# Router logits from column groups of TensorE: the router matrix as the stationary side, and a fold by a 0/1 matrix

## The chip, the cores and the metric

The kernel runs on one core of one Trainium2 chip, in one launch. The metric is the device time of an execution in microseconds (us); the median of several runs is compared. In the profile PE is TensorE (matmul), PEld its weight loads, ACT is ScalarE, DVE is VectorE, POOL is GpSimd, and SP the engine that issues the weight transfers.

## The reference, cut to what matters

A decoder trunk of four layers on 256 tokens of 1024 features, all float32. Each layer has a token mixer (gated DeltaNet, differential attention, gMLP, gated DeltaNet again) and then a mixture of 16 experts with 512 hidden features, of which each token uses two. The router matrix is the same in all layers.

```
def grouped_moe(h, w_router, router_bias, w1, w3, w2):
    scores = sigmoid(h @ w_router)                    # (256, 1024) @ (1024, 16)
    sel = scores + router_bias
    # best of 4 groups by the sum of its two highest; two experts in that group
    # gates = their scores over their sum
    out = sum over e of gates[:, e] * ((silu(h @ w1[e]) * (h @ w3[e])) @ w2[e])

for i in range(4):
    h = layer_norm(ALPHA * h + mixer_i(h))
    h = layer_norm(ALPHA * h + grouped_moe(h))
```

The change touches `h @ w_router` alone.

## The kernel before

Each engine runs a program written out by hand, and the engines meet at semaphores. The eight PSUM banks (128 x 512 float32 each) pass from TensorE to a reader and back: `fill(key)` makes TensorE wait until the bank of that key is drained, `done` reports it filled, `wait_data` lets a reader wait for that, `emptied` reports it drained, and `wait_copy` waits for the drained report. The table behind it, `plan`, counts the turns of each bank in program order. Weights stream from HBM through a ring of six buffers of 2 MB, in the order of their use, and a buffer is loaded again when TensorE is through with it.

Around a router the order is this. Behind the mixer, VectorE normalises the 256 tokens (L986). TensorE turns them into eight chunks of 128 features by 256 tokens, one in each PSUM bank (`ht_chunks`, L1506): first all chunks of the first 128 tokens, then of the second. ScalarE copies the even chunks (L626) and VectorE the odd ones (L946) to HT, with the gain and offset of the norm. For each chunk k TensorE then multiplies it with the router matrix `wr` (L1815), once per half of the tokens: HT is the stationary side (128 columns are loaded), `wr[:, k, :]` the moving side (16 columns are streamed), and the sixteen products add up in bank 0, tokens in the partitions. ScalarE, having copied its chunks, loads its table for exp with a small exp ahead of need (L633), and then takes exp of the 128 x 32 logits (L867). VectorE makes the sigmoid of it, ranks the experts and writes a mask (`route`, L1271 to L1294). TensorE counts with the mask (L1822 to L1824), VectorE turns the counts to places, and TensorE gathers the tokens of the first two experts (L1830) and goes into the loop over eight pairs of experts (L1841 is the first pair of its products, in two column groups of 64: w1 and w3).

Every float32 product shows in the profile as two records, each with its own weight load. A product whose output starts at another partition than 0 uses other columns of the array: a column group.

At the start ScalarE issues some twenty small transfers (L618), the router matrix among the last, and GpSimd sets constants in memory (L508 to L511). A semaphore counts these, `params_in` the transfers.

## Time and profile before

| | us |
|---|---|
| median of 3 runs | 2081.63 (2077.19 to 2081.88) |
| the profiled execution | 2074.54 |
| its span | 2072.8 |
| TensorE busy | 1884.8 (91%) |
| VectorE, ScalarE, GpSimd busy | 718.7, 500.9, 160.6 |

The span runs from the first to the last instruction of the profiled execution. TensorE's clock has two levels, shown as the granted clock: 1.00 is 2.4 GHz, 0.50 is 1.2 GHz; its mean here is 0.943. A router comes four times, near 260, 717, 1255 and 1800 us.

### The profile page before, as it was taken

To read this page: it belongs to the slowest core of one execution; us is meant where nothing else is said; L and a number is where in the kernel's file an instruction comes from. 1 tells how busy PE (TensorE), PEld (TensorE's weight loads), DVE (VectorE), ACT (ScalarE), POOL (GpSimd) and SP (SyncE) were. 2 spreads that over 40 slices of the span, in tenths; PEclk is the share of its full clock that TensorE was granted. 3 is DMA by queue.
4 is the path that set the end of the run, shared out by engine and by line. 5 is a ranking of instruction groups with operands and counts; after the bars stand their busy time and mean duration, and the time that the engine had idled before them with its cause. 6 is when DMAs were issued, how large, how long until landed. Compare 5 with 4: busy or idle time off the path is not lost. (4 is left out here: it accounts for less than half of the span.)

```text
span 2072.8 us, 28488 instructions
## 1 busy us (share of the span) xinstructions
PE 1884.8 (91%) x10610; PEld 1047.6 (51%) x10611; DVE 718.7 (35%) x1433; ACT 500.9 (24%) x1002; POOL 160.6 (8%) x96
## 2 busy tenths in 40 slices
PE   8998979999895789889989997899979988899997
PEld 7858554443763444344434544434438758544442
DVE  3435443232305552223323115232323434543233
ACT  1655221121104111111121101121113745112211
POOL 1112021000300030000020002100002120020000
PEclk9999989999995899989999998899999999889999
DMA  9321149999730266548994424679994330269994
GB/s 356 137 82 64 60 187 410 426 427 404 268 127 35 81 265 260 199 179 356 427 367 148 162 81 174 277 322 423 426 394 155 118 107 3 82 273 428 421 428 194
DMA packets 80056, 504.46 MB, mean 243 GB/s; under 512 B 7171, under 2 KB 11444, under 8 KB 55100
## 3 DMA queue, kind: packets, MB, share of 16 engines
q1 hardware_dynamic: 69808, 488.65, 58.6%
q0 software_dynamic: 2304, 8.39, 1.1%
q10 hardware_dynamic: 7820, 5.65, 0.9%
q8 instruction: 92, 1.51, 0.3%
q14 instruction: 32, 0.26, 0.0%
HBM read 501.61 MB, written 1.06 MB: 243 GB/s over the span
## 5 line engine op out<-in xcount | busy, mean ns | idle before, releaser
L1841 PE MATMUL bank<-ring,work 128*64 128x512 f32 x2176 | 484.3, 603 | 11.6 <-DVE work L1382 6.0
L1841 PEld LDWEIGHTS bank<-ring,work 128*64 128x64 f32 x2176 | 155.6, 139 | 331.0 <-issue 323.8
L1859 PE MATMUL bank<-ring,work 128*64 128x512 f32 x1088 | 244.2, 596 | 9.2 <-ACT work L897 4.6
L1515 PE MATMUL bank<-HT,ring 128*128 128x256 f32 x1024 | 231.3, 386 | 2.9 <-DMA ring<-in_a_w_in 2.9
L1515 PEld LDWEIGHTS bank<-HT,ring 128*128 128x128 f32 x1024 | 198.2, 194 | 39.9 <-issue 10.2
L1523 PE MATMUL bank<-ring,HT 128*128 128x512 f32 x448 | 196.9, 600 | 0.0
L1368 DVE TENSOR_TENSOR work<-bank,work 64x512 f32<-64x512 f32 x64 | 68.0, 1062 | 323.2 <-ACT work L875 323.0
L875 ACT ACTIVATE work<-bank 64x512 f32<-64x512 f32 x64 | 37.8, 590 | 524.7 <-PE bank L1841 524.7
L1830 PE MATMUL bank<-work 128*128 128x128 f32 x1024 | 141.2, 296 | 13.3 <-DVE work L1347 7.1
L1859 PEld LDWEIGHTS bank<-ring,work 128*64 128x64 f32 x1088 | 75.3, 137 | 148.9 <-issue 141.5
L1830 PEld LDWEIGHTS bank<-work 128*128 128x128 f32 x1024 | 129.4, 206 | 38.7 <-issue 29.3
L1523 PEld LDWEIGHTS bank<-ring,HT 128*128 128x128 f32 x448 | 85.8, 193 | 104.8 <-issue 104.7
L1337 DVE TENSOR_TENSOR work<-bank,lncols 128x512 f32<-128x512 f32 x64 | 44.3, 692 | 268.6 <-PE bank L1830 268.6
L1958 PE MATMUL bank<-work 128*128 128x512 f32 x256 | 115.6, 594 | 7.7 <-ACT work L891 5.9
L891 ACT ACTIVATE work<-bank 64x512 f32<-64x512 f32 x128 | 75.8, 592 | 183.3 <-PE bank L1859 182.6
L1062 DVE SCALAR_TENSOR_TENSOR work<-bank,convcols,work 128x255 f32<-128x255 f32 x144 | 69.3, 482 | 105.9 <-ACT work L691 102.5
L1415 DVE TENSOR_TENSOR H<-bank,H 128x512 f32<-128x512 f32 x128 | 84.6, 686 | 52.4 <-PE bank L1958 52.0
L1548 PE MATMUL bank<-ring,work 128*128 128x512 f32 x192 | 85.7, 605 | 0.0
L1958 PEld LDWEIGHTS bank<-work 128*128 128x128 f32 x256 | 46.2, 190 | 57.4 <-issue 57.4
L553 POOL TENSOR_TENSOR H<-H,gB 128x1024 f32<-128x1024 f32 x6 | 14.0, 2356 | 759.8 <-PE bank L1506 759.8
L550 POOL TENSOR_TENSOR H<-work,gB 128x1024 f32<-128x1024 f32 x8 | 23.1, 2905 | 584.2 <-DVE work L1342 584.2
L1548 PEld LDWEIGHTS bank<-ring,work 128*128 128x128 f32 x192 | 36.8, 194 | 44.9 <-issue 44.9
(271 smaller groups left out, 1805.7 us busy)
## 6 DMA issues: line engine op xcount, KB each, us to landing
ring<-in_e_w SPq DMA_DIRECT2D x192, 2048.0 KB, 13.3
ring<-in_a_w_in SPq DMA_DIRECT2D x16, 2048.0 KB, 14.7
ring<-in_c_w_in SPq DMA_DIRECT2D x8, 2048.0 KB, 14.2
ring<-in_b_w_in SPq DMA_DIRECT2D x6, 2048.0 KB, 15.9
ring<-in_a_w_out SPq DMA_DIRECT2D x4, 2048.0 KB, 8.3
ring<-in_c_w_out SPq DMA_DIRECT2D x4, 2048.0 KB, 7.9
ring<-in_b_w_out SPq DMA_DIRECT2D x2, 2048.0 KB, 7.9
gB<-in_ln_mix_g POOLq DMA_DIRECT2D x4, 512.0 KB, 4.2
```

The source lines that it names most:

```text
L891: ins = a(y_[CAP * j:CAP * (j + 1), nh * 512:(nh + 1) * 512], bank[b][nh * CAP:(nh + 1) * CAP, :], ACT.Copy)
L1062: ins = v.scalar_tensor_tensor(dst[:, back:SEQ], ps[:, 0:SEQ - back], convcols[:, j, col:col + 1], dst[:, back:SEQ], ALU.mult, ALU.add)
L1337: v.tensor_tensor(sl, bank[g][:, :].rearrange("p (k c) -> p k c", k=4), lncols[:, g_col + 4 * g:g_col + 4 * g + 4].unsqueeze(2).to_broadca ...
L1368: v.tensor_tensor(by_m(h_[j]), bank[b][CAP:, :], sil[j][CAP:, :], ALU.mult).then_inc(drained[b], 1)
L1415: v.tensor_tensor(part(b), bank[b][:, :], part(b), ALU.add).then_inc(drained[b], 1)
L1515: ins = mm(dst[:, 0:SEQ], wt[:, k, n * P:(n + 1) * P], HT[:, k, :], start=k == 0, stop=k == KC - 1)
L1523: ins = mm(dst[:, :], HT[:, k, tt * P:(tt + 1) * P], wt[:, k, :], start=k == 0, stop=k == KC - 1)
L1548: ins = mm(ps[:, :], turned(h, tt), wts[nh][:, h, :], start=h == 0, stop=h == HEADS - 1)
L1830: ins = mm(bank[g][:, k * 2 * CAP:(k + 1) * 2 * CAP], XH[:, tt, (4 * g + k) * P:(4 * g + k + 1) * P], sel[:, tt, :], start=tt == 0, stop=t ...
L1841: ins = mm(bank[b][lo:lo + CAP, :], x[:, k, :], wt[:, k, :], start=k == 0, stop=k == KC - 1, skip_group_check=True)
L1859: ins = mm(bank[b][nh * CAP:(nh + 1) * CAP, :], h[:, m, :], w2[:, m, nh * 512:(nh + 1) * 512], start=m == 0, stop=m == 3, skip_group_check ...
L1958: mm(bank[b][:, :], selgT[:, tt * P:(tt + 1) * P], y_[:, nh * 512:(nh + 1) * 512], start=True, stop=True).then_inc(filled[b], 1)
```

## The change

The router matrix becomes the stationary side and HT the moving side. Each chunk k is now one product: 32 columns of `wr` are loaded (16 of the matrix and 16 zeros), 256 tokens are streamed, and the result lies in 32 partitions of bank 2, one of four groups by k modulo 4. Chunks k and k + 4 add up in the same group. ScalarE copies the four parts (128 partitions, 256 tokens) to `logitT`. Two products with `logitT` as the stationary side and a 0/1 matrix `fold` as the moving one add the four parts and put the tokens back in the partitions, in bank 0, where exp reads them as before.

```diff
+C_FOLD = C_IOTA + 2 * CAP
+C_SB = C_FOLD + E
...
         if with_moe:
+            turns.take(2, "rtq", i)
             turns.take(0, "rt", i)
...
-        wr = sb("wr", [P, KC, E])
+        wr = sb("wr", [P, KC, 2 * E])
...
+        logitT = work[:, 6144:6144 + SEQ]
...
+            pool.memset(wr[:, :, E:], 0.0).then_inc(consts_set, 1)
...
-            small.append((wr[:, :, :], w["w_router"].rearrange("(p k) n -> p k n", p=P)))
+            small.append((wr[:, :, 0:E], w["w_router"].rearrange("(p k) n -> p k n", p=P)))
...
-            act.wait_ge(consts_set, 4)
+            act.wait_ge(consts_set, 5)
...
             def experts(i):
                 ahead(ACT.Exp)
+                emptied(a(logitT, wait_data(act, "rtq", i)[:, 0:SEQ], ACT.Copy), "rtq", i)
                 emptied(a(rt[:, 0, :], wait_data(act, "rt", i)[:, 0:TT * E], ACT.Exp, scale=-1.0), "rt", i)
...
-                ps = fill("rt", i)
+                ps = fill("rtq", i)
                 for k in range(KC):
                     wait_copy(pe, "ht", 2 * i + 1, k)
-                    for tt in range(TT):
-                        ins = mm(ps[:, tt * E:(tt + 1) * E], HT[:, k, tt * P:(tt + 1) * P], wr[:, k, :],
-                                 start=k == 0 and tt == 0, stop=k == KC - 1, skip_group_check=True)
+                    q = slice(2 * E * (k % 4), 2 * E * (k % 4 + 1))
+                    ins = mm(ps[q, 0:SEQ], wr[:, k, :], HT[:, k, :], start=k < 4, stop=k >= 4, skip_group_check=True)
+                done(ins, "rtq", i)
+                ps = fill("rt", i)
+                wait_copy(pe, "rtq", i)
+                for tt in range(TT):
+                    ins = mm(ps[:, tt * E:(tt + 1) * E], logitT[:, tt * P:(tt + 1) * P], fold, start=True, stop=True)
                 done(ins, "rt", i)
...
+    c[:, C_FOLD:C_FOLD + E] = m % (2 * E) == np.arange(E)[None, :]
```

Word for word, TensorE's order at the first router, before: the last transposes, the sixteen router products (the first eight rows of them are shown), each `drained` being the bank of a chunk that must have been copied.

```order
L1506 MATMUL bank<-consts_sb,work 128x128 [waits xhat_ready]
L1506 MATMUL bank<-consts_sb,work 128x128 x3
L1815 MATMUL bank<-wr,HT 128x16 [waits drained0]
L1815 MATMUL bank<-wr,HT 128x16
L1815 MATMUL bank<-wr,HT 128x16 [waits drained1]
L1815 MATMUL bank<-wr,HT 128x16
L1815 MATMUL bank<-wr,HT 128x16 [waits drained2]
L1815 MATMUL bank<-wr,HT 128x16
L1815 MATMUL bank<-wr,HT 128x16 [waits drained3]
L1815 MATMUL bank<-wr,HT 128x16
```

The same place on TensorE now (line numbers are those of the changed kernel; L1832 is the first product with the mask):

```order
L1512 MATMUL bank<-consts_sb,work 128x128 x3
L1821 MATMUL bank<-HT,wr 32x256 [waits drained0,drained2]
L1821 MATMUL bank<-HT,wr 32x256 [waits drained1]
L1821 MATMUL bank<-HT,wr 32x256 [waits drained2]
L1821 MATMUL bank<-HT,wr 32x256 [waits drained3]
L1821 MATMUL bank<-HT,wr 32x256 [waits drained4]
L1821 MATMUL bank<-HT,wr 32x256 [waits drained5]
L1821 MATMUL bank<-HT,wr 32x256 [waits drained6]
L1821 MATMUL bank<-HT,wr 32x256 [waits drained7]
L1826 MATMUL bank<-consts_sb,work 128x16 [waits drained2,drained0]
L1826 MATMUL bank<-consts_sb,work 128x16
L1832 MATMUL bank<-work,consts_sb 128x32 [waits mask_ready,drained1]
```

Sixteen products have become eight and two; the first now waits for bank 2 too, and the two folding products wait for ScalarE's copy (`drained2`).

ScalarE at the same place before: its last two chunks, the table load, and the exp of the logits.

```order
L626 ACTIVATE HT<-bank,lncols 128x256 [waits filled4]
L626 ACTIVATE HT<-bank,lncols 128x256 [waits filled6]
L633 ACT_TABLE_LOAD
L633 ACTIVATE warm<-epsc 128x1
L867 ACTIVATE work<-bank 128x32 [waits filled0,a_chain]
```

ScalarE now:

```order
L631 ACTIVATE HT<-bank,lncols 128x256 [waits filled4]
L631 ACTIVATE HT<-bank,lncols 128x256 [waits filled6]
L638 ACT_TABLE_LOAD
L638 ACTIVATE warm<-epsc 128x1
L872 ACTIVATE work<-bank 128x256 [waits filled2,a_chain]
L873 ACTIVATE work<-bank 128x32 [waits filled0]
```

The copy (L872) stands between the warm-up and the exp, and no further table load comes with it.

## Rows read from the trace of the kernel before

**Rows 1.** Page: busy time of each engine, share of the span, instructions.

```profile
PE 1884.8 (91%) x10610; PEld 1047.6 (51%) x10611; DVE 718.7 (35%) x1433; ACT 500.9 (24%) x1002; POOL 160.6 (8%) x96
```

**Rows 2.** Chain of waits, layer 3's router: start us, us, what.

```profile
1800.75 5.61 PE bank L1815 x32
```

**Rows 3.** Timeline, layer 0's router: start us, us, instructions [idle before].

```profile
259.41 1.93 ACT L626 ACTIVATE HT<-bank,lncols 128x256 f32<-128x256 f32 x4 [2.11 <-PE bank L1506]
...
260.65 6.85 PE L1815 MATMUL bank<-wr,HT 128*128 128x16 f32 x32
...
262.65 0.20 ACT L633 ACTIVATE warm<-epsc 128x1 f32<-128x1 f32 x1
267.60 0.20 ACT L867 ACTIVATE work<-bank 128x32 f32<-128x32 f32 x1 [4.74 <-PE bank L1815]
```

**Rows 4.** Timeline, layer 1, from the router to the first experts.

```profile
716.14 1.93 ACT L626 ACTIVATE HT<-bank,lncols 128x256 f32<-128x256 f32 x4 [1.98 <-PE bank L1506]
...
716.92 4.27 PE L1815 MATMUL bank<-wr,HT 128*128 128x16 f32 x32
...
719.38 0.20 ACT L633 ACTIVATE warm<-epsc 128x1 f32<-128x1 f32 x1
721.28 0.20 ACT L867 ACTIVATE work<-bank 128x32 f32<-128x32 f32 x1 [1.70 <-PE bank L1815]
...
725.42 0.50 PEld L1822 LDWEIGHTS bank<-work,consts_sb 128*128 128x128 f32 x2 [4.35 <-issue]
...
726.23 0.55 PEld L1824 LDWEIGHTS bank<-work,ones 128*128 128x128 f32 x2
...
726.99 0.16 DVE L1304 CAST counts<-bank 1x16 int32<-1x16 f32 x1 [0.81 <-PE bank L1824]
...
728.56 6.14 PE L1830 MATMUL bank<-work 128*128 128x128 f32 x32 [1.67 <-DVE work L1347]
...
734.62 3.65 PE L1841 MATMUL bank<-ring,work 128*64 128x512 f32 x16
```

**Rows 5.** Timeline, layer 2's router.

```profile
1253.99 1.93 ACT L626 ACTIVATE HT<-bank,lncols 128x256 f32<-128x256 f32 x4 [1.98 <-PE bank L1506]
...
1257.24 0.20 ACT L633 ACTIVATE warm<-epsc 128x1 f32<-128x1 f32 x1
1260.94 0.20 ACT L867 ACTIVATE work<-bank 128x32 f32<-128x32 f32 x1 [3.50 <-PE bank L1815]
```

**Rows 6.** Timeline, layer 3's router.

```profile
1799.79 1.93 ACT L626 ACTIVATE HT<-bank,lncols 128x256 f32<-128x256 f32 x4 [1.98 <-PE bank L1506]
...
1803.04 0.20 ACT L633 ACTIVATE warm<-epsc 128x1 f32<-128x1 f32 x1
1806.44 0.20 ACT L867 ACTIVATE work<-bank 128x32 f32<-128x32 f32 x1 [3.20 <-PE bank L1815]
```

**Rows 7.** Stretches: length, busy us of each engine, granted clock, DMA share, GB/s.

```profile
718.00:720.00 2.00, 2.00 (x19) 2.00 (x19) 0.18 (x1) 1.56 (x3) 0.00 (x0) 0.94 0.37 156
1254.00:1256.00 2.00, 1.99 (x18) 1.75 (x16) 2.00 (x5) 1.98 (x5) 0.00 (x0) 0.91 1.01 434
1800.00:1802.00 2.00, 1.99 (x18) 1.91 (x17) 1.85 (x5) 1.98 (x5) 0.00 (x0) 0.94 1.03 442
```

**Rows 8.** Line L1515 in 14.4:19 and 35.8:43.9: ns min/median/max, first and last start.

```profile
L1515 PE MATMUL bank<-HT,ring x11: 634/634/796, 14.4 to 18.8; 128*128 128x256 f32 x11
...
L1515 PE MATMUL bank<-HT,ring x39: 379/379/379, 35.6 to 43.8; 128*128 128x256 f32 x39
```

**Rows 9.** Page, costliest groups: busy us, mean ns of one, idle before.

```profile
L1841 PE MATMUL bank<-ring,work 128*64 128x512 f32 x2176 | 484.3, 603 | 11.6 <-DVE work L1382 6.0
```

**Rows 10.** Line L773 in 1700:1730: a copy of 128x256 on ScalarE.

```profile
L773 ACT ACTIVATE work<-bank x2: 385/385/385, 1721.0 to 1721.5; 128x256 f32<-128x256 f32 x2
```

**Rows 11.** Timeline at the start of the kernel: GpSimd's first squares.

```profile
33.48 1.04 POOL L565 TENSOR_TENSOR work<-work 128x512 f32<-128x512 f32 x1 [17.85 <-DMA rel<-in_rel_bias]
...
35.60 1.04 POOL L565 TENSOR_TENSOR work<-work 128x512 f32<-128x512 f32 x1 [1.08 <-ACT work L681]
```

More of the change, by code:

```diff
@@ L58 @@
 C_IOTA = C_CD + 2 * E
-C_SB = C_IOTA + 2 * CAP
+C_FOLD = C_IOTA + 2 * CAP
+C_SB = C_FOLD + E
 C_OH = C_SB
@@ L227, in trunk @@
         tri = K_[:, C_TRI:C_TRI + P]
+        fold = K_[:, C_FOLD:C_FOLD + E]
         onehot = bB[0:REL_BUCKETS + 1, 0:TOEP]
@@ L1971, in _ @@
             pe.wait_ge(rows_for_cols, N_ROWS)
-            pe.wait_ge(consts_set, 4)
+            pe.wait_ge(consts_set, 5)
             ps = fill("cols")
```

## The prediction, made before the changed kernel ran

> **What bounds the kernel now.** I read four views in this order. First the page's busy times: TensorE (PE) is busy 91% of the span, 1884.8 us [rows 1]. That average doesn't say what the router logits are worth, so next the chain of waits at a router, in layer 3: the router products (L1815) stand in it with 5.61 us, nothing beside them [rows 2]. The work behind them is a string of short VectorE steps that all wait for ScalarE's exp (L867), so each microsecond by which that exp starts earlier is one of the whole. Third, the timeline at each of the four routers, for what ScalarE does meanwhile [rows 3 to 6]. The exp starts at 267.60, 721.28, 1260.94 and 1806.44 us; ScalarE has been free, its exp table warm (end of the 0.20 us at L633), since 262.85, 719.58, 1257.44 and 1803.24. The gaps are 4.75, 1.70, 3.50 and 3.20 us, 13.15 together: the most that any faster router product can give, before anything is added.
>
> The gaps differ because TensorE's clock does. In layer 0 the 32 records of L1815 take 6.85 us, 0.21 each; in layer 1 they take 4.27 [rows 3, 4]. The fourth view, stretches of 2 us with the granted clock, says why: 0.94 over 718 to 720 is the full level (1.00, 2.4 GHz) until 719.76 and the low one (0.50, 1.2 GHz) after it; 0.91 over 1254 to 1256 puts the fall at 1255.64, 0.94 over 1800 to 1802 at 1801.76 [rows 7]. Layer 0's block is as slow throughout as the low level makes it.
>
> Does the expert stage behind the router take a gain back? TensorE's waits there name VectorE, ScalarE and issue, no DMA. A router that ends earlier moves everything behind it earlier, the release of weight buffers too.
>
> **The change, part by part.** Removed per layer: 16 products, 32 records, each loading 128 columns of HT and streaming 16 of the router matrix. Added on TensorE: 8 products (16 records) that load 32 columns and stream 256, in four column groups in turn, and then two 128x16 products (4 records) that fold. Added on ScalarE between them: a copy of 128x256 out of PSUM, queued behind the table load and warm-up, with the exp behind it. Moved: the first router product now waits for bank 2 too, so for ScalarE's second HT chunk, where it waited for the first only.
>
> *A 256-column record.* At the low clock one lasts 634 ns, at the full clock 379, and there 39 start in 8.2 us, 0.216 each [rows 8]. Eleven at the low clock start over 4.4 us, 0.44 each, with one odd one among them; twice the full pitch is 0.43. I use 0.427 and 0.214. That is the price where one waits for the other.
>
> *Do column groups overlap?* The experts' products (L1841) alternate two groups of 64 columns, 512 streamed. Their 2176 records keep TensorE busy for 484.3 us, 0.223 each, though one lasts 603 ns and a record of 512 columns alone in the array would hold it twice 0.214 [rows 9]. So two run at a time. A product has two records in the same group, and they are issued in order, so what overlaps is the second half of one product with the first half of the next. Four groups in turn have the same order; I take one product per record time, 0.427 low or 0.214 full: twice as fast as in a row, not four times.
>
> *Start.* ScalarE's four chunks take 1.93 us at some 0.57 each, so pitch 0.455, and the second ends 1.02 after the first starts. In layer 1 the first chunk ended about 716.71 and the first product began at 716.92 [rows 4]: 0.2 us. New start: first chunk's start + 1.22.
>
> *Tail.* If TensorE ends last: 0.10 to ScalarE, 0.385 for a copy of this size [rows 10], 0.10 back, and the fold. For the fold rows 4 have four equal records at the low clock, loads from 725.42 to 726.23, 0.81 us, for two products; the reader of the last pair comes 0.76 after that pair's first load, so two products cost 0.81/2 + 0.76 = 1.17 us. Sum 1.75. If ScalarE ends last: 0.02 + 0.385 + 0.10 + 1.17 = 1.67 after its table is warm. The later of the two sets the exp. The copy could cost up to the 0.57 of an HT chunk, which carries a scale and a bias: 0.2 more per layer, 0.7 in all. I take 0.385, the like operation.
>
> - Layer 0, low clock: start 260.63, eighth product 7 x 0.427 later at 263.62, its second record 264.05, end 264.68, exp 266.43. Before 267.60: -1.17 us.
> - Layer 1, full clock: start 717.36, last record 719.07, end 719.45; ScalarE is free only at 719.58, exp 721.25. Before 721.28: -0.03.
> - Layer 2: start 1255.21, two products until the fall, then low: last record 1258.2, end 1258.84, exp 1260.59. Before 1260.94: -0.35.
> - Layer 3: start 1801.01, three and a half products until the fall: last record 1803.68, end 1804.31, exp 1806.06. Before 1806.44: -0.38.
>
> Sum -1.9 us. Of the 5 to 7 us block that went, most is given back by the later start (0.46 a layer), the copy (0.385) and the fold (1.17).
>
> *A switch between one array and column groups* comes twice per layer more. The trace has such a switch between the gather (L1830, 128 columns, ends 734.70) and the experts' first product (64 columns, starts 734.62): the next starts before the last ends [rows 4], so I take 0. Upper bound: the 0.2 us by which a record outlasts its pitch at the low clock (634 - 427 ns), eight times, 1.7 us. The Trainium skill (TensorEngine Tiling (Array Packing), Key Properties) says that changing the tiling mode drains TensorE; by that rule the sum would be about -0.2 instead of -1.9. The row shows no stop of that size.
>
> *At the start* the router matrix lands in pieces of 16 elements instead of runs of 128, the constants grow by 16 columns, and GpSimd gets one more memset. The last parameter lands before 33.48 us, where GpSimd begins its squares; its second squares begin at 35.60, after waiting 1.08 us for ScalarE [rows 11]. A landing up to 1 us later is hidden by that wait. Beyond it GpSimd still has most of its time free, and TensorE and ScalarE ask for parameters after 40 us. Bounds 0 and +1; I take 0.
>
> **Against the measured time.** The profiled execution took 2074.54 us for a span of 2072.8, so the sum makes 2072.6 of it. The median shown is 2081.63, 7 us above (2077.19 to 2081.88). Forecast: 2081.63 - 1.9 = 2079.7 us. About 0.3%, 6.2 us, is what a measurement of this kernel tells from no change.
>
> **Rivals.**
> 1. *The column groups don't overlap* (slower). Sixteen records stand in a row, full pitch until the fall, low after it: the last starts at 267.04, 721.4, 1261.2 and 1806.7; with 0.634 and 1.75 the exp is at 269.4, 723.8, 1263.6 and 1809.1: +1.8, +2.5, +2.6, +2.6 = +9.5 us, 2091.1. For it: nothing in this trace runs four groups, or groups of 32 columns. Against: two groups do overlap. It decides from a low-clock pitch per product of 0.427 + 1.9/28 = 0.50 us (seven steps in each of four layers), where the gain is gone; at 0.72 it is beyond 0.3%.
> 2. *The dense streaming keeps the clock up* (faster). The old block streams 16 columns a record, and the clock fell within it in three layers. If the new block runs at 2.4 GHz, ScalarE's queue alone sets the exp, 1.67 after its table is warm: 264.52, 721.25, 1259.11, 1804.91: -3.1, 0, -1.8, -1.5 = -6.4 us, 2075.2. With the fold at the full clock too, its four pitches and its last record take some 0.5 us less each: -8.4, 2073.2. Against it: the low level holds from the very beginning of layer 0's block, in a stretch that isn't touched, and the idle gaps before and behind the block stay. The Trainium skill (TensorE: Matmul & The Clock Gate, Part 1) says that the clock is throttled by default and that activity releases it, which is this rival's ground.
> 3. *The later start, the copy and the fold eat exactly what the products give*: no difference, 2081.6. All its parts are in the forecast; 1.9 us more of them are enough (the drain alone would be). For a reader of times it is the forecast's own answer.
>
> A spread, not a rival: where the clock rises again behind the router moves from one execution to the next. A record costs up to 0.1 us more at the low level [rows 3, 4], some 15 records per layer are at stake, so 1 to 2 us of either sign in a layer, and 2 in a median.
>
> **Chances.** Forecast 0.60, rival 3 0.21, rival 1 0.10, rival 2 0.09. Rival 2 passes the 0.3% with its first part just barely and with both; the spread can carry the forecast over it a few times in a hundred; of rival 1 nearly all lies beyond it. Faster 0.11, same 0.78, slower 0.11. The range runs from rival 2's far end to half way to rival 1: 2073.8 to 2086.0 us; the forecast's own is 2077 to 2083.
>
> **What would show it.** Right: first product behind ScalarE's second chunk; sixteen records within about 3.5 us at the low clock, one product every 0.43; the copy 0.4 us long; from copy to exp 1.3 us; in layer 1 the copy right behind the warm-up. Wrong: records 0.43 apart (rival 1); a granted clock of 1.00 through the blocks of layers 2 and 3 (rival 2); records of one product overlapping, or three products at a time, which would make the block shorter than I allow and leave ScalarE as the only bound; a gap of half a microsecond between transposes and router products (the drain); TensorE waiting for parameters in the first 60 us.

## The result, and the profile after

| | before | after |
|---|---|---|
| median of 9 runs, us | 2077.19 (2073.31 to 2081.88) | 2065.57 (2060.59 to 2073.05) |
| span of the profiled execution, us | 2072.8 | 2058.8 |
| four routers, ScalarE's first HT copy to its exp, us | 26.9 | 19.0 |

The ratio is 0.9932 [0.9909, 0.9954]: 0.7% faster, 11.6 us between the medians and 14.0 between the spans. The forecast was 2079.7 us, with a range down to 2073.8. It started from 2081.63, the median of three runs, where nine give 2077.19; beyond that its gain of 1.9 us is some 10 us too small.

The page after: TensorE's busy time fell by 18 us from that of [rows 1], and it has 48 records fewer.

```profile
span 2058.8 us, 28401 instructions
PE 1866.4 (91%) x10562; PEld 1024.9 (50%) x10563; DVE 717.8 (35%) x1433; ACT 502.1 (24%) x1006; POOL 160.0 (8%) x97
...
L1851 PE MATMUL bank<-ring,work 128*64 128x512 f32 x2176 | 485.3, 604 | 12.0 <-DVE work L1388 6.0
```

The experts' products are what they were [rows 9]. Now the timeline at layer 0's router, which answers to [rows 3] (start us, length, instructions, in brackets the idle time before and what ended it; L1821 is the new block, L872 the copy, L1826 the fold, L873 the exp):

```profile
261.36 1.93 ACT L631 ACTIVATE HT<-bank,lncols 128x256 f32<-128x256 f32 x4 [1.97 <-PE bank L1512]
262.43 0.27 PEld L1821 LDWEIGHTS bank<-HT,wr 128*32 128x32 f32 x8 [0.35 <-ACT HT L631]
262.43 1.65 PE L1821 MATMUL bank<-HT,wr 128*32 128x256 f32 x16
...
264.60 0.20 ACT L638 ACTIVATE warm<-epsc 128x1 f32<-128x1 f32 x1
264.84 0.38 ACT L872 ACTIVATE work<-bank 128x256 f32<-128x256 f32 x1
265.37 0.59 PE L1826 MATMUL bank<-consts_sb,work 128*128 128x16 f32 x4 [1.28 <-ACT work L872]
265.99 0.20 ACT L873 ACTIVATE work<-bank 128x32 f32<-128x32 f32 x1 [0.77 <-PE bank L1826]
...
273.35 6.58 PE L1840 MATMUL bank<-work 128*128 128x128 f32 x32 [1.76 <-DVE work L1353]
```

All sixteen records are through in 1.65 us, 0.1 us a record on average; the old block took 6.85. TensorE ends at 264.08, before ScalarE is free at 264.80. From there copy, fold and exp follow in 1.19 us. In layer 2 the clock falls within the block; this answers to [rows 5]:

```profile
1248.09 2.10 PE L1821 MATMUL bank<-HT,wr 128*32 128x256 f32 x16
...
1250.27 0.20 ACT L638 ACTIVATE warm<-epsc 128x1 f32<-128x1 f32 x1
1250.50 0.38 ACT L872 ACTIVATE work<-bank 128x256 f32<-128x256 f32 x1
1251.03 1.00 PE L1826 MATMUL bank<-consts_sb,work 128*128 128x16 f32 x4 [0.83 <-ACT work L872]
1252.07 0.20 ACT L873 ACTIVATE work<-bank 128x32 f32<-128x32 f32 x1 [1.18 <-PE bank L1826]
```

Even here the block ends (1250.19) before ScalarE is free (1250.47); only the fold is slower, 1.00 instead of 0.59. The granted clock, as in [rows 7] (after the clock: DMA share, GB/s):

```profile
262.00:264.00 2.00, 1.89 (x19) 0.87 (x17) 1.41 (x4) 1.98 (x4) 0.00 (x0) 1.00 0.98 418
...
1247.00:1249.00 2.00, 1.87 (x18) 1.08 (x17) 2.00 (x5) 1.96 (x5) 0.00 (x0) 0.88 1.01 434
1250.00:1252.00 2.00, 1.17 (x6) 0.92 (x4) 0.00 (x0) 0.84 (x3) 0.00 (x0) 0.50 1.05 451
...
1786.00:1788.00 2.00, 1.87 (x20) 1.20 (x20) 1.78 (x4) 1.98 (x5) 0.00 (x0) 1.00 1.05 451
```

Full level (1.00, 2.4 GHz) through the block in layers 0 and 3, where the old block had the low one all through or from 1801.76 on; in layer 2 it falls to 1.2 GHz within the block. Layer 1 is the other way round: its block begins at the low level, which by the two stretches lasts until about 719.45, and yet takes 1.68 us:

```profile
716.27 1.57 PEld L1512 LDWEIGHTS bank<-consts_sb,work 128*128 128x128 f32 x8 [1.83 <-DVE work L992]
...
716.78 1.93 ACT L631 ACTIVATE HT<-bank,lncols 128x256 f32<-128x256 f32 x4 [2.12 <-PE bank L1512]
...
718.17 0.20 PEld L1821 LDWEIGHTS bank<-HT,wr 128*32 128x32 f32 x8 [0.33 <-ACT HT L631]
718.17 1.68 PE L1821 MATMUL bank<-HT,wr 128*32 128x256 f32 x16
```

```profile
716.00:718.00 2.00, 1.73 (x8) 1.57 (x8) 1.88 (x5) 1.22 (x3) 0.00 (x0) 0.51 1.05 451
...
718.00:720.00 2.00, 1.85 (x18) 0.77 (x16) 0.90 (x2) 1.98 (x3) 0.00 (x0) 0.64 0.56 238
```

Where the 14.0 us went, from the timelines and windows of the two traces (in brackets the same for a second pair of executions, whose spans differ by 17.7):

| stage | before | after | difference |
|---|---|---|---|
| start to layer 0's router | 259.4 | 261.4 | +2.0 (+4.0) |
| four routers, first HT copy to exp | 26.9 | 19.0 | -7.9 (-9.1) |
| exp to the experts' first product | 53.4 | 54.1 | +0.7 (0.0) |
| experts | 1117.4 | 1111.8 | -5.6 (-9.6) |
| mixers | 615.6 | 612.7 | -2.9 (-2.9) |

Two things call for an explanation: 8 us at the router where 1.9 were forecast, and 8 to 12 us less in the stages behind the routers, among instructions that the change doesn't touch.

### The profile page after: what moved, and what is told of

Same layout as the page of the kernel before. It is cut to its first block and busy times, and to the rows that moved or that the text cites. A ratio compares the mean times of both kernels' runs of the same rounds, so it can differ in the third digit from the quotient of the medians.

```text
span 2058.8 us, 28401 instructions
## 1 busy us (share of the span) xinstructions
PE 1866.4 (91%) x10562; PEld 1024.9 (50%) x10563; DVE 717.8 (35%) x1433; ACT 502.1 (24%) x1006; POOL 160.0 (8%) x97
## 5 line engine op out<-in xcount | busy, mean ns | idle before, releaser
L1869 PE MATMUL bank<-ring,work 128*64 128x512 f32 x1088 | 245.5, 602 | 7.5 <-ACT work L903 4.6
L1869 PEld LDWEIGHTS bank<-ring,work 128*64 128x64 f32 x1088 | 76.7, 138 | 147.2 <-issue 139.7
## 6 DMA issues: line engine op xcount, KB each, us to landing
ring<-in_c_w_in SPq DMA_DIRECT2D x8, 2048.0 KB, 12.5
```

The source lines that it names most:

```text
L1869: ins = mm(bank[b][nh * CAP:(nh + 1) * CAP, :], h[:, m, :], w2[:, m, nh * 512:(nh + 1) * 512], start=m == 0, stop=m == 3, skip_group_check ...
```

## The experiments

Ratios are to before, from runs of the same job, with their 95% interval. "Router" is the second row of the table above.

### How many column groups

The change unchanged, and again with one and two groups of 32 columns in place of four; copy and fold are then of 32 or 64 partitions. The number of instructions doesn't change.

```diff
-q = slice(2 * E * (k % 4), 2 * E * (k % 4 + 1))
-ins = mm(ps[q, 0:SEQ], wr[:, k, :], HT[:, k, :], start=k < 4, stop=k >= 4, ...)
+q = slice(2 * E * (k % n), 2 * E * (k % n + 1))          # n = 1, n = 2
+ins = mm(ps[q, 0:SEQ], wr[:, k, :], HT[:, k, :], start=k < n, stop=k >= KC - n, ...)
```

> The changed kernel once more, beside the three variants of this series. The first execution moved the exp of the router, counted from ScalarE's first HT copy, from 8.19, 5.15, 6.95 and 6.65 us to 4.63, 4.63, 5.05 and 4.63: 8.0 us of the 14 by which the span fell; the other 6 us are spread over stretches that run the same instructions. Theory A (only the router block changed, and the other 6 us are where the clock's low stretches happened to fall): again 4.6 to 5.1 us per layer, a total 8 to 11 us below the kernel before. Theory B (the block also changes the clock of what follows, for good): 12 to 15 us below, and less low-clock time behind the routers in this trace too.

> All eight router products in the same column group of 32, so that nothing in the block can overlap; the copy and the fold take 32 partitions instead of 128. Theory 'the groups are what pays': sixteen records at 0.214 us (full clock) from 1.07 us after ScalarE's first copy on, end at 4.7, exp at 6.0 us at the full clock and up to 9.9 at the low one, against 4.6 to 5.1: 6 to 14 us slower than the changed kernel, near the kernel before. Rival 'it is the clock': dense streaming of 256 columns keeps the clock at 1.00 and the exp stays within 1.5 us per layer of the changed kernel, under 6 us in all.

> Two column groups instead of four; copy and fold take 64 partitions. If each group holds one record at a time and groups are free of each other, records start in twos, the block takes about 1.9 us at the full clock and ends before ScalarE's table is warm, so the exp stays at 4.6 us; at the low clock it ends about 4.7 us after the first copy and the exp comes at 6.4 instead of 5.0. Sum 0 to 4 us slower than the changed kernel. If, as I had forecast, a product's second half must go before the next product's first, two and four groups give the same block: no difference at either clock.

| groups | median us | ratio | router us | block at the full clock, us |
|---|---|---|---|---|
| 4 | 2065.27 | 0.9924 [0.9897, 0.9951] | 19.0 | 1.65 |
| 2 | 2064.58 | 0.9913 [0.9888, 0.9939] | 21.1 | 1.92 |
| 1 | 2075.06 | 0.9975 [0.9953, 0.9997] | 25.0 | 3.64 |

The kernel of after came out 16 us below before in this series. The theory that the untouched stages change by chance gave 8 to 11, the one that the block also changes the clock of what follows gave 12 to 15; TensorE's time at the low level is 217 us in this trace and 206 in the first, against 237 and 234 in the two traces of before.

Timeline of layer 1 with one group, then layers 1 and 2 with two:

```profile
716.60 3.64 PE L1821 MATMUL bank<-HT,wr 128*32 128x256 f32 x16
...
718.77 0.20 ACT L638 ACTIVATE warm<-epsc 128x1 f32<-128x1 f32 x1
720.33 0.37 ACT L872 ACTIVATE work<-bank 32x256 f32<-32x256 f32 x1 [1.36 <-PE bank L1821]
721.47 0.20 ACT L873 ACTIVATE work<-bank 128x32 f32<-128x32 f32 x1 [0.77 <-PE bank L1826]
```

```profile
722.45 1.92 PE L1821 MATMUL bank<-HT,wr 128*32 128x256 f32 x16
...
1252.24 3.31 PE L1821 MATMUL bank<-HT,wr 128*32 128x256 f32 x16
...
1255.65 0.38 ACT L872 ACTIVATE work<-bank 64x256 f32<-64x256 f32 x1 [1.04 <-PE bank L1821]
```

With one group ScalarE has the table warm at 718.97 and waits 1.36 us for TensorE; sixteen records at 0.214 and the last one's length make the 3.64. With two groups the block takes 1.92 at the full clock. Going from one group to four saves 6.0 us of router. From two to four it saves 2.1, because only where the clock is low does the shorter block still matter (3.31 us long in layer 2, ScalarE waits 1.04); the times of the two kernels don't differ. (The profiled execution of two_groups was 11 us longer than its median; I read nothing of it but the router and one pair of experts.)

So four groups do better than the two records at a time of the forecast, which would put the last start 7 x 0.214 = 1.5 us behind the first and the end at 1.9, what two groups take. How much better shows where the low level slows the array down. In layer 1 of after four records start within 0.02 us, the next four 0.43 us later, and so on. In the second trace of after (after_again) the whole block of layer 0 runs at the low level, and takes 1.94 us:

```profile
264.87 1.94 PE L1821 MATMUL bank<-HT,wr 128*32 128x256 f32 x16
```

```profile
264.00:266.00 2.00, 2.00 (x17) 1.32 (x19) 1.60 (x4) 1.98 (x5) 0.00 (x0) 0.50 0.99 426
```

Four products, not one, share a record time of 0.43 us, and both halves of a product do so. At the full clock the array isn't even the limit: the last four products of layer 0 each start some 0.05 us after their HT chunk is copied, so the 1.65 us are the pace of ScalarE's and VectorE's chunks. The Trainium skill (TensorEngine Tiling (Array Packing), Key Properties) says that tiles run independently, loads and products in parallel; the starts in fours agree with it.

One group alone changes the router by -1.9 to -3.1 us, and is 0.25% (5 us) faster. The interval of that ratio takes in 2 to 3 us as well, so it is no more than a hint at a second cause.

### ScalarE's copy moved to VectorE

```diff
-                emptied(a(logitT, wait_data(act, "rtq", i)[:, 0:SEQ], ACT.Copy), "rtq", i)
 ...
+                emptied(v.tensor_copy(logitT, wait_data(dve, "rtq", i)[:, 0:SEQ]), "rtq", i)
                 route(i)
```

> The copy of the four parts goes to VectorE, which is idle there, instead of ScalarE behind its table load. Theory 'ScalarE's queue is the bound now': block end 2.7 us after the first copy, plus 0.1, 0.42 (a copy of this size on VectorE), 0.1 and the fold 0.7 to 1.1: exp at 4.1 instead of 4.6 us, 2 us faster in all than the changed kernel. Rival 'TensorE's block or the fold is the bound': no difference in the exp's start.

Measured 2068.03 us, 0.9941 [0.9917, 0.9966]. Timeline of layer 1:

```profile
717.56 1.65 PE L1821 MATMUL bank<-HT,wr 128*32 128x256 f32 x16
...
719.25 0.42 DVE L1321 COPY work<-bank 128x256 f32<-128x256 f32 x1 [0.71 <-PE bank L1821]
719.73 0.20 ACT L638 ACTIVATE warm<-epsc 128x1 f32<-128x1 f32 x1
720.51 0.20 ACT L872 ACTIVATE work<-bank 128x32 f32<-128x32 f32 x1 [0.57 <-PE bank L1826]
```

VectorE copies while ScalarE still warms its table, and the exp comes 0.58 after the table instead of 1.19. The router falls from 19.0 to 16.5 us: ScalarE's queue was the bound in all four layers. But the time doesn't follow: where 2 us less than after was expected, no difference can be measured. A router time alone doesn't set the time of this kernel to within 3 us.

### Before, once more

> The kernel before, unchanged, for a second trace and the noise. All theories: ratio 1.000 within its interval. If the router block of before is really set by TensorE's weight loads, the exp comes 5 to 8.2 us after ScalarE's first HT copy in each layer, whatever the place of the clock's low stretches; if a value under 5 appears, the first trace was an unlucky one and the gain of the change is smaller than 8 us. The stretch up to the first router took 259.4 us against 260.5 to 266.5 in the five executions with the change: if the small transfers at the start cost something, this trace is again near 259; if it is chance, it lies among the others.

2080.31 against 2080.22 us, 1.0007 [0.9988, 1.0025]; router 28.1 us. Its four routers take 4.75, 8.19, 7.05 and 8.15 us where the first trace has 8.19, 5.15, 6.95 and 6.65; the sum is near, the layers change places. Those of after are 4.63, 4.63, 5.05 and 4.63 in both of its traces. The 4.75 is the old block at the full clock but for its last 0.6 us:

```profile
260.30 3.85 PE L1815 MATMUL bank<-wr,HT 128*128 128x16 f32 x32
```

Where the old block has the full clock, then, the change saves 0.1 us of router; where it has the low one throughout, 3.6. The new router takes 4.63 us at either level (layer 0 of after and of after_again). Four routers of 4.75 us would be 19.0, the sum of after: the 8 us are what the low clock cost the old block.

### Products that only keep TensorE busy

Ten products of 256 columns into a bank that nothing reads, seven behind the fold and three behind the ranks, while TensorE waits for VectorE; in before, in after, and in the version with VectorE's copy. The last kernel has four of 512 columns instead.

```diff
                 done(ins, "rt", i)
+                for _ in range(7):
+                    mm(bank[7][:, 0:SEQ], ones[:, :], K_[:, 0:SEQ], start=True, stop=True)
 ...
+                for _ in range(3):
+                    mm(bank[7][:, 0:SEQ], ones[:, :], K_[:, 0:SEQ], start=True, stop=True)
                 first = at[("moe", i)]
```

> The kernel before with products that nobody needs in TensorE's idle time of each router: seven of 128x256 behind the router products (while VectorE ranks) and three behind the ranks (they write a free bank). Theory 'the low clock behind the routers is the engine's idleness': the gather runs at the full clock, 4.1 us instead of 5.9 per layer, 6 to 7 us less in all, minus up to 2 us where the seven products, at the low clock, outlast VectorE's chain. Rival 'the clock there is chance': no difference.

> The same seven and three products in the changed kernel. If dense streaming keeps the clock up, it enters the idle time at 1.00 and stays there: gather 4.1 us instead of 5.6 to 6.5, ranks 0.4 us shorter: 7 to 10 us less than the changed kernel, about 2057 us where that has 2065. Rival: the clock falls anyway within the block of seven, and what they delay eats the gain: within 2 us of the changed kernel.

> After_fill with the copy on VectorE: exp 0.6 us earlier per layer as copy_dve's trace showed (4.02 instead of 4.63), so 2 us less than after_fill. If the times of copy_dve (2068 where the changed kernel had 2065) mean that VectorE's copy costs something later on, it is again slower than its partner by some 3 us.

> Filling products again, but three of 512 columns and one instead of seven and three of 256: 16 more instructions a layer than the changed kernel instead of 40, 2.6 and 0.85 us of streaming at the full clock. The clock theory expects from fold to experts the 6.7 + 3.9 us of after_fill instead of 7.3 + 6.0. Theory L adds only that the waits of the expert loops come out as some other mixture: 2055 to 2066 us. Without L it should be 8 us under the changed kernel, 2057.

| kernel | median us | ratio | router | exp to experts | experts |
|---|---|---|---|---|---|
| before_fill | 2084.96 | 1.0015 [0.9996, 1.0035] | 30.1 | 45.8 | 1125.8 |
| after_fill | 2071.42 | 0.9946 [0.9927, 0.9964] | 18.5 | 42.6 | 1125.2 |
| dve_fill | 2069.29 | 0.9928 [0.9901, 0.9954] | 17.5 | 42.9 | 1127.9 |
| after_fill512 | 2070.14 | 0.9929 [0.9907, 0.9952] | 19.0 | 43.9 | 1128.3 |

Timeline of after_fill, layer 3 (L1829 and L1877 the added products, L1842 the gather):

```profile
1801.28 3.27 PE L1829 MATMUL bank<-consts_sb,ones 128*128 128x256 f32 x14
...
1806.30 1.54 PE L1877 MATMUL bank<-consts_sb,ones 128*128 128x256 f32 x6
1808.12 3.84 PE L1842 MATMUL bank<-work 128*128 128x128 f32 x32 [0.28 <-DVE work L1353]
```

The gather runs at the full clock, 3.84 us instead of the 5.6 to 6.6 of after, and exp to experts shrinks by 11 us. None of it arrives: after_fill was expected near 2057 us and isn't faster than after, and its experts' stage is 9 to 13 us longer than in the two traces of after. Most of that is TensorE's busy time (6 to 11 us more over the same products), with 89 us at the low level in that stage instead of 69 and 80; the waits that the profile calls "issue" (the engine waited for nothing that it shows) grow by 1 to 2 us. So the experts' stage isn't independent of what stands ahead of it.

### Padding: more instructions, nothing else

N products of 32 x 8 behind the fold, into the same unread bank: 4 instructions each (two loads, two matmuls). The change removes 24 instructions per layer, so N = 6 puts the number of before back, and N = 10 has as many as after_fill.

```diff
                 done(ins, "rt", i)
+                for _ in range(N):
+                    mm(bank[7][0:32, 0:8], ones[:, 0:32], K_[:, 0:8], start=True, stop=True)
```

> Two of the short products, 8 more instructions a layer. Theory L: the short first pairs of 25.9 us in layers 1 and 2 may be kept or lost, one of them at least differs from after_pad6 or the changed kernel, and the time lies between 2060 and 2072. Rival C: no difference to the changed kernel, 2065 within 2 us.

> The changed kernel with six products of 32 columns by 8 behind the fold, in the 4.3 us in which TensorE waits for VectorE's ranks: 24 more instructions a layer, as many as the change took out, so that from there on the program lies where it lay before. They are short enough not to delay the ranks. In both traces of the kernel before, the first pair of experts in layers 1 and 2 took 29.9 to 32.3 us; in all five of the change and its variants with as few instructions 25.9 to 26.6; in the three with the filling products 29.4 to 31.5. Theory L (where the program's instructions lie decides at which branches TensorE waits for them): first pairs of layers 1 and 2 back at 30 us and some 3 to 9 us slower than the changed kernel, 2068 to 2074 us. Rival C (the clock's phase, or the earlier exp, makes them short): 25.9 us as in the changed kernel, same time.

> Ten of the short products, 40 more instructions a layer: the same place for the program as in after_fill, without the clock that the long ones kept up. Theory L: first pairs of layers 1 and 2 at 30 us, last pairs at 33 to 35 as in after_fill, and a time 7 to 10 us above after_fill (2071), about 2079 us, though TensorE's routers are those of the changed kernel. Rival C: as the changed kernel, 2065.

> The kernel before with six of the short products behind the router products of each layer, in TensorE's wait for the ranks: nothing on the path to the exp. Theory L (the place of the program decides part of the time): the experts' first and last pairs come out otherwise than in the kernel before, and the time differs from it by up to 8 us of either sign. Rival: what the short products cost in after_pad6 and after_pad10 is theirs alone (they delay the ranks or lower the clock): then also the kernel before gets 8 to 10 us slower, with first and last pairs as before.

| kernel | instructions per layer against before | median us | ratio | router |
|---|---|---|---|---|
| after | -24 | 2065.27 | 0.9924 [0.9897, 0.9951] | 19.0 |
| after_pad2 | -16 | 2070.11 | 0.9948 [0.9927, 0.9968] | 18.5 |
| after_pad6 | 0 | 2075.84 | 0.9961 [0.9938, 0.9983] | 19.0 |
| after_pad10 | +16 | 2080.63 | 0.9990 [0.9967, 1.0013] | 18.5 |
| before_pad6 | +24 | 2090.62 | 1.0050 [1.0027, 1.0073] | 24.7 |

Timeline of after_pad10, layer 3:

```profile
1813.78 0.80 PE L1829 MATMUL bank<-consts_sb,ones 128*32 128x8 f32 x20
1813.89 0.20 ACT L873 ACTIVATE work<-bank 128x32 f32<-128x32 f32 x1 [0.77 <-PE bank L1826]
...
1818.05 0.61 PE L1834 MATMUL bank<-work,consts_sb 128*128 128x32 f32 x2 [3.47 <-DVE work L1300]
```

The padding is over in 0.8 us, beside the exp, and TensorE then waits 3.47 us for VectorE: on the spot it costs nothing, and the router keeps its 4.63 us in every layer. Yet the whole gain is gone. It is hardly the clock: over all executions the mean granted clock is 0.947 to 0.948 in after, 0.947 in after_pad6 and 0.946 in after_pad10, and within one kernel 0.001 of it goes with some 1.3 us. One place where the time goes is the first pair of experts. TensorE in layer 1, before, after and after_pad10 in turn (before's L1859 is after's L1869):

```profile
751.13 0.72 PE L1830 MATMUL bank<-work 128*128 128x128 f32 x5 [0.48 <-issue]
...
752.27 3.65 PE L1859 MATMUL bank<-ring,work 128*64 128x512 f32 x16
...
758.87 1.94 PE L1859 MATMUL bank<-ring,work 128*64 128x512 f32 x8 [2.94 <-issue]
```

```profile
749.09 2.05 PE L1840 MATMUL bank<-work 128*128 128x128 f32 x16
...
751.57 7.09 PE L1869 MATMUL bank<-ring,work 128*64 128x512 f32 x32
```

```profile
761.57 0.33 PE L1860 MATMUL bank<-consts_sb,work 128*128 128x128 f32 x1 [2.66 <-issue]
...
774.51 3.47 PE L1842 MATMUL bank<-work 128*128 128x128 f32 x16 [2.55 <-issue]
```

Windows over that whole first pair of experts, before and after:

```profile
734.62:765.10 30.48, 26.57 (x140) 11.41 (x140) 15.89 (x14) 4.78 (x11) 11.64 (x6) 1.00 0.71 287
```

```profile
734.55:760.40 25.85, 25.85 (x139) 11.24 (x139) 15.86 (x14) 4.65 (x10) 11.62 (x6) 1.00 0.65 262
```

Same work, same clock, but before has 3.91 us in which TensorE has no record, all of it "issue" (0.48 and 2.94 in the rows, 0.49 once more at 764.21), and after has none. In after_pad10 5.2 of the 7.0 us that the pair is longer than in after are "issue"; there the clock is low for 3.4 us too. Over all kernels the length of this pair goes with the program, not with the router:

| layer 1, first pair | us |
|---|---|
| before, before_again | 30.5, 30.6 |
| after, one_group, two_groups, copy_dve and the two staged versions below without filling | 25.9 each |
| after_pad2, after_pad6, after_pad10 | 26.1, 30.4, 32.9 |
| before_fill, after_fill, dve_fill, after_fill512 | 29.6, 30.4, 31.5, 30.1 |
| stage_dve_fill (16 instructions fewer than before) | 25.9 |
| before_pad6 | 31.5 |

With 16 or 24 instructions fewer than before the pair takes 26 us, with 8 fewer, as many or more 29.6 to 32.9. But this pair isn't the whole stage. From before to after the first pairs of all four layers together lose 7.3 us (11.7 in the second traces) and the last pairs gain 5.3 (7.3). Over the whole execution TensorE's "issue" waits are 23.9 and 26.4 us in the two traces of before, 26.9 and 26.1 in after, 30.2 in after_pad6, 33.6 in after_pad10 and 31.6 in before_pad6. before_pad6 is 0.50% slower than before (10 us, where up to 8 of either sign were expected). By the rival, that the short products cost something only where they stand, its first and last pairs had to be as before; its last pairs are 13 us longer in all.

So this much is shown: instructions that cost nothing where they stand, added to TensorE's program, make the kernel slower, in three doses in after and once in before. With the number of before the change keeps 0.39% of its 0.76%, some 8 us, which is what the routers gave. That the other half came by taking 24 instructions out follows from this comparison alone; the "issue" waits didn't become fewer from before to after, what fell in the experts' stage is TensorE's busy time (by 4 to 5 us, with 6 us less at the low level).

What TensorE waits for in these gaps the traces do say in part. The page has a DMA queue "q8 instruction", which moved 92 pieces of 16 KB in before. Over all 18 traces 206 "issue" waits of TensorE are longer than 1 us, and 197 of them end 1.2 to 2.4 us after the last landing of such a piece; of 990 equally long waits for another engine or a DMA it is 49. The 2.94 us of before lie around the piece that starts at 756.4. TensorE's instructions arriving late is what this points to, and a longer program shifts where the pieces end. It's a match in time; no run varied it by itself.

The fill kernels now read differently. after_fill and after_pad10 have equally many instructions; they differ by 9.2 us in median, and by 9.7 in exp to experts. The full clock for the gather is worth its 9 us, and 40 more instructions per layer, with the clock that the experts' stage loses, cost as much.

### The start of the kernel

The router matrix lands whole, in runs of 128 elements as before, in a tile of its own; GpSimd spreads it.

```diff
-small.append((wr[:, :, 0:E], w["w_router"]...))
+small.append((wr0[:, :, :], w["w_router"]...))
             pool.wait_ge(params_in, N_PARAMS)
+            pool.tensor_copy(wr[:, :, 0:E], wr0[:, :, :]).then_inc(consts_set, 1)
```

(TensorE waits for that sixth count at its first router.) Then the same with VectorE's copy, and that with two filling products of 512 columns.

> The changed kernel with one part undone: the router matrix lands in one run per partition, in a tile of its own, and GpSimd copies it to its places among the zeros once the parameters are in. In the five and more traces of the change GpSimd's first squares start at 38.7 to 39.9 us instead of 33.5 to 34.3, and the token products of the first gate begin at 112.9 us at the earliest instead of 111.9 to 112.5. Theory S (the scattered landing costs): squares at 34 us, first router 1 to 2 us earlier than in the change's traces, a time 1 to 2 us less. Rival (hidden, as I had forecast): squares earlier, the rest as it is.

> After_stage with the copy of the four parts on VectorE. By what the traces show of each part: exp at 4.0 us instead of 4.6 per layer (-2.4 us) and -1 us at the start, so 3 us below the changed kernel. As the changed kernel and copy_dve differ by +3 us where the parts say -2, I expect the place of ScalarE's and VectorE's programs to matter by as much: 2058 to 2068.

> Stage_dve with two products of 512 columns behind the fold, 8 more instructions a layer, 1.7 us of streaming at the full clock. If that is enough to keep the clock at 1.00 into the gather, gather and ranks are 2.5 us shorter a layer, 10 us in all; it is less than the 3.0 and 2.6 us that did. 2052 to 2066 us.

| kernel | median us | ratio | to layer 0's router | router |
|---|---|---|---|---|
| after_stage | 2062.69 | 0.9920 [0.9889, 0.9951] | 259.4 | 18.9 |
| stage_dve | 2065.74 | 0.9915 [0.9885, 0.9944] | 258.9 | 16.9 |
| stage_dve_fill | 2066.32 | 0.9929 [0.9906, 0.9952] | 261.8 | 16.6 |

GpSimd at the start, after and then after_stage, which answer to [rows 11]:

```profile
39.32 2.04 POOL L570 TENSOR_TENSOR work<-work 128x512 f32<-128x512 f32 x2 [23.94 <-DMA rel<-in_rel_bias]
```

```profile
34.45 0.29 POOL L588 COPY wr<-wr 128x128 f32<-128x128 f32 x1 [18.83 <-DMA rel<-in_rel_bias]
34.71 2.03 POOL L571 TENSOR_TENSOR work<-work 128x512 f32<-128x512 f32 x2
```

The last parameter lands near 39 us in after against 33.5 before, and near 34.4 with the whole matrix landing at once; the start stage falls by 2 us in the profiled executions. Its length also varies with the clock (259.9 to 269.4 us over the traces with the scattered landing), so TensorE's idle time up to the router is the better measure: 24.1 and 24.5 us in the traces of before, 25.7 and 25.9 in after, 24.5 in after_stage. The scattered landing costs some 1.5 us. after_stage has the lowest median, 2062.69 (2058.04 to 2071.13), and the shortest span, 2056.1. That it beats after isn't shown: the intervals overlap almost wholly. VectorE's copy on top brings nothing again, and the two filling products in stage_dve_fill, expected to bring up to 10 us, shorten exp to experts by 2 us and the time not at all.

## Why the prediction was wrong, step by step

**The overlap of column groups** is the step that failed: "I take one product per record time, 0.427 low or 0.214 full: twice as fast as in a row, not four times." The expert stage, with two groups, allowed both "two records at a time" and "as many as there are groups"; I argued from the order of a product's halves that four groups could do no better than two. It was four times: at the low level the block took 1.94 us (layer 0 of after_again), where the forecast had about 3.5 for the sixteen records; at the full one 1.65, the pace of the HT chunks. The prediction had named this outcome as a sign ("three products at a time, which would make the block shorter than I allow and leave ScalarE as the only bound"), and gave it no case and no chance. With ScalarE the bound in every layer my own numbers give -6.4 us (rival 2's sum), whatever the clock of the block.

**The clock.** Rival 2 (0.09) came half true: layers 0 and 3 had 1.00 through the block, layer 2 fell within it, and layer 1 had the low level for the first 1.3 of its 1.68 us. It didn't matter to the exp, since TensorE ended before ScalarE in all four. In layers 0, 1 and 3 the fold ran at the full clock: 1.19 us from warm table to exp where I had 1.67. In layer 2 it is 1.60. That is 3 x 0.48 + 0.07 = 1.5 us, and with the -6.4 makes the -7.9 of the table. One group, sixteen records in a row, had 1.00 throughout layer 1's block as well:

```profile
716.00:718.00 2.00, 1.89 (x11) 1.02 (x11) 1.59 (x4) 1.98 (x5) 0.00 (x0) 1.00 1.02 434
718.00:720.00 2.00, 2.00 (x11) 0.91 (x9) 0.00 (x0) 0.96 (x2) 0.00 (x0) 1.00 0.04 16
```

But its phase moves by itself: layer 0's router begins at the low level in before and in after_again, at the full one in after and in before_again. Over all executions after and its variants without padding or filling have a mean granted clock of 0.946 to 0.949, before has 0.942; by the 1.3 us for 0.001, some 7 of the 11 to 16 us go with it, the routers' own share included. Whether the dense block raised it or the shorter low stretches of a faster router count for it stays open.

**Copy and start of the block: right.** Copy 0.38 (forecast 0.385), from copy to exp 1.15; first load 1.07 after ScalarE's first HT copy at the full clock, 1.4 at the low one (1.22 forecast).

**Mode switch: 0 in the time, but not in the trace.** At the full clock TensorE's first load in 32-column groups starts 0.05 us after ScalarE's second HT chunk, so nothing of a stop shows. At the low level it does: in layer 1 of after the chunk is copied by 717.81 and the last load of the transposes over by 717.84, and the first load comes at 718.17, 0.33 us later; all blocks that begin at the low level have this gap. In before, without a switch, the first router load at the low level starts right with the end of the transposes' last (layer 0: within 0.02 us). The rule of the Trainium skill that was weighed there (TensorEngine Tiling (Array Packing), Key Properties: changing the mode drains TensorE) agrees with these 0.3 us. The row that spoke against it doesn't: the next record's start 0.08 us before the last one's end is what layer 1 shows as well (718.17 and 718.24), with the stop in it. The stop is longer than the 0.2 us that the prediction allowed for as its bound. It cost nothing because ScalarE ended last.

**Rival 1** (no overlap, +9.5) is refuted twice: by the overlap, and by one_group, where the products do stand in a row and the kernel is still not slower, since sixteen records at the full clock cost 3.64 us.

**The start** was mis-sized: 0, bound +1. The last landing moved by 5 us, not by up to 1, and the stage is 2.0 us longer, some 1.5 of it TensorE's idle time; after_stage gives the 2.0 back in its trace.

**What I had no term for**: the number of instructions. The forecast took the stages behind the router as fixed in length. They lost 7.8 us in this pair of traces (+0.7, -5.6, -2.9), 12.5 in the other, and by the padding 24 instructions per layer account for about half of the gain: after_pad6 is 0.37% above after, at the same mean clock. The page of before had the hint, "issue" as a cause of idle in the experts' stage, and I noted it without a price.

**The range** has slips of its own: rival 2's far end, -8.4, is 2073.2 and not 2073.8, and half way to rival 1 is 2085.4 and not 2086.0. The result lies below both.

The sum, worked out afterwards (an estimate): routers -8, start +2, and 96 instructions at (2080.63 - 2065.27) / 160 = 0.10 us each, -9: -15 us. Measured between the medians are -11.6 here and -16 in the second job. The price per instruction comes from adding them, and is used here for taking them out. It's good to some 4 us only: two_groups, with 2 us more of router than after, should be slower and isn't; copy_dve should be faster and isn't.

## What to carry to other kernels

- Count the column groups of a product: with few stationary columns, groups in turn ran side by side here, two as well as four. Ask next which engine then ends last; beyond that point more groups, or a faster copy, bring nothing (two groups did here what four do).
- Price a block at both levels of the clock. The old router took 4.75 to 8.2 us by the level it met, the new block cost the router nothing at either (4.63 us, 5.05 where the fold was slow too); that was the whole gain there.
- A gain at one place is to be compared with a kernel of equal instruction count. Where the profile names "issue" on the bounding engine, instructions elsewhere in its program have a price, and idle-time fillers may pay it too.
- A small constant that lands in short runs can delay the whole first stage. Land it whole and spread it on an idle engine.

## What the runs showed of the hardware

- Four groups of 32 columns, 128 rows, fp32: sixteen records of 256 columns in 1.94 us at the low level of the clock, four starting together every 0.43 us; at the full one 1.65 us (set by the chunks they wait for), 1.92 in two groups, 3.64 in one.
- From 128-column transposes to 32-column groups the next load came 0.33 us late at the low level of the clock (layer 1 of after).
- More instructions in TensorE's program made "issue" waits longer elsewhere: 24 more per layer made one pair of experts 4.5 us longer (25.9 to 30.4 us) at an unchanged clock, 40 more 7.0, of which 5.2 are "issue". Of the 206 "issue" waits over 1 us in the 18 traces 197 end 1.2 to 2.4 us after a 16 KB piece of the queue "q8 instruction" has landed.
- Filling TensorE's wait behind the router with 256-column products made the gather of 32 records take 3.84 us instead of 5.6 to 6.6.
